# Row maximum of masked attention taken as a minimum of negatively scaled scores, signalled per tile

## The chip, the cores and the metric

The kernel runs on one NeuronCore of one Trainium2 chip. The metric is the device time of one execution in microseconds (us); lower is better.

## The reference, cut to what matters

Two transformer blocks run one after the other on 256 tokens of width 1024, in float32. They hold four attentions. Three are masked and hold 32 heads together: a causal block attention with 8 heads of 64 (`moba`), an attention over selected keys with 8 heads of 64 (`dsa`), and a latent attention with 16 heads of 96 (`mla`). The fourth, a cross attention with 4 heads of 256 (`cross`), has no mask. For each head and query the reference computes

```
logits = (q . k) * scale, masked entries -inf (or -1e30)
p      = softmax(logits)        # exp(logits - max) / sum
out    = p @ v
```

Around them lie projections, norms, retention, a short convolution and three feed-forward layers, which are matrix products against 176 MB of weights.

## The kernel before, in words

Each engine has a hand-written program, and semaphores order them. The 256 tokens are two tiles (t = 0, 1) of 128 rows. Weights stream through a ring: SyncE issues the loads (L379), ScalarE makes the rounded high part (`w_hi`, L572), VectorE the remainder (`w_lo`, L981 and L983), and TensorE multiplies three products of high and low parts (L1468). A weight unit's slot is released when TensorE has used it (`w_used`), and the raw slot when VectorE has made the low part (`w_low`).

An attention is a pipeline over heads, written once for all four (`attention` in each engine's program):

- TensorE: `scores(hd)` (L1572, one bank of PSUM, 128 columns for tile 0 and 256 for tile 1), then `turn_probs(hd-2)` (L1580, three transposes), then `values(hd-3)` (L1589, six products in the masked attentions). `scores(hd)` waits until the bank of head hd-2 is free (`maxed`).
- VectorE: `masked_max(hd)` makes two tensor_tensor_reduce (L1127), one for each tile: scores plus mask into the SBUF tile `S`, and the row maximum into `mx`. In the trace each is a CUSTOM_DVE_ANT_0 followed by a DVE_READ_ACCUMULATOR2_ANT. It then waits for its own two marks and makes the bias `nb = -scale * mx` for both tiles with one tensor_scalar of 2 columns (L1134, SBUF to SBUF), which raises `maxed` by 1. Behind it in the same queue stands `copy_turned(hd-2)` (L1140, PSUM to SBUF, 384 columns), on which `values` waits.
- ScalarE: for each head it waits on `maxed`, then makes `E = exp(scale * S + nb)` for tile 0 and tile 1 with row sums (L733), and signals `probs`. `turn_probs` waits on that.

In `moba` the first two heads stand inside a projection. ScalarE's program is: weight splits, head 0, one split (L572), the eviction of tile 0 (L631), head 1, the eviction of tile 1 (L631), then the other heads. VectorE's is: head 0, one split (L981), then the rest. TensorE waits for both evictions before `scores(3)`. In `mla` ScalarE has splits ahead of heads 2 and 4, VectorE ahead of heads 4 and 6. In `dsa` GpSimd runs the convolution at the same time (`convolve`, L500 to L504: tensor_tensor on SBUF tiles of 128x1024). Its result goes through ScalarE (L911) and VectorE (L1391) after the attention; TensorE's next projection waits for these.

The non-masked attention (`cross`) takes one tensor_reduce from PSUM (L1131) and the same tensor_scalar (L1134).

Of the kernel before, what the change touches and what calls it, by code (L numbers as in the profile page):

```python
# [19 lines left out]
ALU = mybir.AluOpType  # L20
# [5 lines left out]
TT = SEQ // P  # L26
# [3 lines left out]
PICKED = -3e38  # L30
# [65 lines left out]
def rows_stat(b, t):  # L96
    return added(b, t) + TT


def block_kernel(nc, A, out):  # L100

    with ExitStack() as ctx:
# [32 lines left out]
        PS = ctx.enter_context(nc.psum_tensor("PS", [P, 8, 512], F32))  # L135
# [63 lines left out]
        def out_banks(a, t):  # L199

            return PS[:, a.out_bank + t, :] if a.H * a.dv == 512 else acc(t).rearrange("p a b -> p (a b)")
# [354 lines left out]
        def _(act):  # L556
# [19 lines left out]
            def split_to(u):  # L576
                while n["split"] <= min(u, COUNT - 1):
                    split(n["split"])
                    n["split"] += 1

            def by_rows(stat):

                act.wait_ge(rstd_ready, stat + 1)
                return rstd[:, stat:stat + 1]
# [138 lines left out]
            def attention(a, heads=None, splits=True):  # L723
                for hd in heads or range(a.H):
                    if splits and hd in (2, 4):
                        split_to(min(n["split"], n["used"] + 1))
                    act.wait_ge(a.maxed, hd + 1)
                    if hd >= 3:
                        act.wait_ge(a.turned, hd - 2)
                    for t in range(TT):  # L730
                        c0, c1 = a.cols[t]
                        src = a.S[hd % 3][:, c0:c1] if a.masked else PS[:, a.score_bank + hd % 2, c0:c1]
                        ins = act.activation(a.E[hd % 3][:, c0:c1], src, ACT.Exp, bias=a.nb[:, hd, t:t + 1],  # L733
                                             scale=a.scale, accum_out=a.sums[:, hd, t:t + 1])
                    ins.then_inc(a.probs, 1)

            def whole(tile, width=512):
# [104 lines left out]
            n["used"] += 4  # L842
            split_to(n["used"] + 1)
            attention(moba, [0])
            split_to(n["used"] + 2)
            evict(0, rows2(k_tok), mem_rows)
            attention(moba, [1])
            evict(1, rows2(k_tok), mem_rows)
            attention(moba, range(2, moba.H), False)
            split_to(n["used"] + 3)  # L850
            high_banks(2, half_rows(hT_hi, 0))
# [71 lines left out]
            for t in range(TT):  # L923
                wait_acc(t)
                scale = by_rows(rows_stat(4, t))
# [40 lines left out]
        def _(dve):  # L966
            steps = Steps(dve, dve_step)
# [19 lines left out]
            def split_to(u):  # L987
                while n["split"] <= min(u, COUNT - 1):
                    split(n["split"])
                    n["split"] += 1  # L990
# [128 lines left out]
            def attention(a, heads=None, splits=True, rows=None):  # L1119
                def masked_max(hd):  # L1120
                    dve.wait_ge(a.scores, hd + 1)
                    if hd >= 3:
                        dve.wait_ge(a.probs, hd - 2)
                    if a.masked:
                        for t in range(TT):
                            c0, c1 = a.cols[t]
                            steps.mark(dve.tensor_tensor_reduce(  # L1127
                                out=a.S[hd % 3][:, c0:c1], in0=PS[:, a.score_bank + hd % 2, c0:c1], in1=a.mask[t], scale=1.0,
                                scalar=PICKED, op0=ALU.add, op1=ALU.max, accum_out=a.mx[:, hd, t:t + 1]))
                    else:  # L1130
                        steps.mark(dve.tensor_reduce(a.mx[:, hd, :], PS[:, a.score_bank + hd % 2, :].rearrange("p (t s) -> p t s", t=TT),  # L1131
                                                     AX, ALU.max))
                    steps.wait()
                    dve.tensor_scalar(a.nb[:, hd, :], a.mx[:, hd, :], -a.scale, None, ALU.mult).then_inc(a.maxed, 1)  # L1134

                def copy_turned(hd):
                    dve.wait_ge(a.turned, hd + 1)
                    if hd >= 2:
                        dve.wait_ge(a.summed, hd - 1)
                    dve.tensor_copy(a.ET[hd % 2], PS[:, a.prob_bank + hd % 2, 0:a.cols[1][1]]).then_inc(a.copied, 1)  # L1140

                for hd in heads or range(a.H + 2):
                    if splits and hd in (4, 6):
                        split_to(min(n["split"], n["used"] + 1))
                    if hd < a.H:
                        masked_max(hd)
                    elif rows is not None:
                        normalise_half(a, rows, hd - a.H, 0)
                    if hd >= 2:
                        copy_turned(hd - 2)  # L1150

            def normalise_half(a, dst, t, half):

                heads = slice(half * a.H // 2, (half + 1) * a.H // 2)
                if t == 0:
                    dve.wait_ge(a.summed, heads.stop)
                    steps.link(dve.reciprocal(a.sums[:, heads, :], a.sums[:, heads, :]))
                dve.tensor_tensor(dst[:, t, 512 * half:512 * half + 512].rearrange("p (h d) -> p h d", d=a.dv),
                                  PS[:, 2 * t + half, :].rearrange("p (h d) -> p h d", d=a.dv),
                                  a.sums[:, heads, t:t + 1].to_broadcast([P, a.H // 2, a.dv]), ALU.mult).then_inc(h_ready, 1)  # L1160
# [140 lines left out]
            for t in range(TT):  # L1301
                for hd in range(4):
                    cols, stat = slice(128 * hd, 128 * hd + 128), RETENTION + 4 * t + hd
                    ins = dve.scalar_tensor_tensor(out=mix[:, t, 512 + cols.start:512 + cols.stop], in0=PS[:, 2 + t, cols],
                                                   scalar=rstd[:, stat:stat + 1], in1=sil[:, t, cols], op0=ALU.mult, op1=ALU.mult)
# [98 lines left out]
            for t in range(TT):  # L1404
                dve.wait_ge(ss_ready, LATENTS + 2 * t + 2)
                s = rows_stat(4, t)
# [41 lines left out]
        def _(pe):  # L1448
# [115 lines left out]
            def attention(a, heads=None, rows=None):  # L1564
                def scores(hd):
                    if hd >= 2:
                        pe.wait_ge(a.maxed if a.masked else a.probs, hd - 1)
                    for t in range(TT):
                        c0, c1 = a.cols[t]
                        pairs = list(zip(a.q(hd, t * P, (t + 1) * P), a.k(hd, 0, c1 - c0)))  # L1570
                        for i, (q, k) in enumerate(pairs):
                            mm = pe.matmul(PS[:, a.score_bank + hd % 2, c0:c1], q, k, start=i == 0, stop=i == len(pairs) - 1)  # L1572
                    mm.then_inc(a.scores, 1)

                def turn_probs(hd):
                    pe.wait_ge(a.probs, hd + 1)
                    if hd >= 2:
                        pe.wait_ge(a.copied, hd - 1)
                    for b in range(a.cols[1][1] // P):
                        mm = pe.transpose(PS[:, a.prob_bank + hd % 2, b * P:(b + 1) * P], a.E[hd % 3][:, b * P:(b + 1) * P], ident[:])  # L1580
                    mm.then_inc(a.turned, 1)

                def values(hd):
                    pe.wait_ge(a.copied, hd + 1)
                    for t in range(TT):
                        c0, c1 = a.cols[t]
                        blocks = (c1 - c0) // P
                        for s in range(blocks):
                            mm = pe.matmul(out_banks(a, t)[:, hd * a.dv:(hd + 1) * a.dv], a.ET[hd % 2][:, c0 + s * P:c0 + (s + 1) * P],  # L1589
                                           a.v(hd, s), start=s == 0, stop=s == blocks - 1)  # L1590
                    mm.then_inc(a.summed, 1)

                for hd in heads or range(a.H + 3):
                    if hd < a.H:
                        scores(hd)
                    if 2 <= hd < a.H + 2:
                        turn_probs(hd - 2)
                    if hd >= 3:
                        values(hd - 3)
                    if rows is not None and hd == a.H + 1:  # L1600
                        turn_half(rows, 0)

            def turn_half(tile, at):

                for t in range(TT):
                    wait_h()
                    turn([tile[:, t, at + P * b:at + P * (b + 1)] for b in range(4)])
# [369 lines left out]
```

## Time and profile before

| what | value |
|---|---|
| median of 3 runs | 1088.29 us (1087.21 to 1093.13) |
| the profiled execution's own time | 1089.14 us |
| its span in the profile | 1087.3 us |
| granted TensorE clock, mean | 0.991 |
| TensorE (PE) matmul busy | 1044.9 us, 96% |
| VectorE (DVE) busy | 655.1 us, 60% |
| ScalarE (ACT) busy | 564.1 us, 52% |
| GpSimd (POOL) busy | 99.8 us, 9% |

The profile is of one execution. Times are us from the span's start unless marked ns. Busy time of matmuls is modelled from their starts, so 96% doesn't mean the peak rate. The span leaves out some 2 us around the program (1089.14 against 1087.3). The `moba` attention lies at 99 to 121 us, `dsa` at 550 to 572, `mla` at 841 to 873.

### The profile page before, as it was taken

Reading aid. Unit: us, or ns where it says so; the run is one execution under the profiler, and the core shown is the slowest. Engines: PE = TensorE matmul, PEld = TensorE weight load, DVE = VectorE, ACT = ScalarE, POOL = GpSimd, SP = SyncE. Lnnn points to the kernel's source line nnn. Section 1 sums busy time; section 2 is a strip of 40 time slices with the busy share of each in tenths; the row PEclk is TensorE's granted clock in tenths of the full one; section 3 lists DMA queues with packets and bytes.
Section 4 is the critical chain, followed back from the end, with each engine's and each line's share of the span. In section 5 each row is a group of like instructions: output and inputs, shape, how many; then the busy total and the mean of one; then the engine's idle time right before and its main releaser. Section 6 shows DMA issues by size and latency. Waiting matters only on the chain.

```text
span 1087.3 us, 13860 instructions
## 1 busy us (share of the span) xinstructions
PE 1044.9 (96%) x5080; PEld 872.4 (80%) x5080; DVE 655.1 (60%) x1020; ACT 564.1 (52%) x855; POOL 99.8 (9%) x127
## 2 busy tenths in 40 slices
PE   7999999999999999999979999999997999999997
PEld 6887878887888887878867888888886878888886
DVE  5575665456565555647876755545654867555453
ACT  6566455437454455644544744454454647445541
POOL 2010110001000001104440100000140001000000
PEclk9999999999999999999989999999999999999999
DMA  8746136215545545633422655554252225555521
GB/s 336 279 174 230 58 117 219 110 58 183 204 159 190 215 149 187 237 136 118 152 75 103 234 188 196 188 192 153 70 190 105 78 92 221 191 195 190 193 78 39
DMA packets 28462, 176.31 MB, mean 162 GB/s; under 512 B 3248, under 2 KB 3392, under 8 KB 9984
## 3 DMA queue, kind: packets, MB, share of 16 engines
q1 hardware_dynamic: 26784, 170.08, 43.2%
q0 software_dynamic: 1456, 5.48, 1.4%
q8 instruction: 30, 0.49, 0.2%
q10 hardware_dynamic: 176, 0.13, 0.0%
q14 instruction: 16, 0.13, 0.0%
HBM read 174.62 MB, written 1.05 MB: 162 GB/s over the span
## 4 chain that ended last, share of the span: by engine, by line
PE 82%; DVE 9%; ACT 3%; issue 3%; POOL 2%; DMA 1%; SPq 0%; DVEq 0%; ACTq 0%; POOLq 0%
PE PS L1468 71%; PE PS L1537 3%; DVE w_lo L983 3%; PE PS L1589 2%; PE PS L1572 2%; ACT w_hi L572 2%; PE PS L1679 2%; DVE w_lo L981 1%; DMA x<-in_x 1%; DVE work L1127 1%; POOL h L487 1%; PE PS L1580 1%; DVE h L1347 1%; POOL arena L480 1%; ACT work L653 0%
## 5 line engine op out<-in xcount | busy, mean ns | idle before, releaser
L983 DVE SCALAR_TENSOR_TENSOR w_lo<-w_raw,gcol,w_hi 128x512 fp32r<-128x512 f32 (+4 forms) x322 | 269.4, 895 | 208.4 <-ACT w_hi L572 207.8
L572 ACT ACTIVATE w_hi<-w_raw,gcol 128x512 fp32r<-128x512 f32 (+4 forms) x322 | 243.4, 824 | 99.4 <-PE PS L1468 98.5
L1468 PE MATMUL PS<-w_hi,hT_hi 128*128 128x512 f32 (+3 forms) x904 | 246.4, 393 | 7.8 <-DVE hT_lo L998 3.0
L1468 PE MATMUL PS<-w_hi,hT_lo 128*128 128x512 f32 (+3 forms) x904 | 240.2, 386 | 0.0
L1468 PE MATMUL PS<-w_lo,hT_hi 128*128 128x512 f32 (+3 forms) x904 | 238.9, 385 | 0.9 <-DVE w_lo L983 0.8
L1468 PEld LDWEIGHTS PS<-w_lo,hT_hi 128*128 128x128 f32 x904 | 167.5, 188 | 35.9 <-DVE w_lo L983 2.4
L1468 PEld LDWEIGHTS PS<-w_hi,hT_hi 128*128 128x128 f32 x904 | 164.0, 189 | 40.1 <-issue 3.8
L1468 PEld LDWEIGHTS PS<-w_hi,hT_lo 128*128 128x128 f32 x904 | 168.1, 189 | 33.2
L981 DVE TENSOR_TENSOR w_lo<-w_raw,w_hi 128x2048 fp32r<-128x2048 f32 (+1 forms) x70 | 135.7, 1954 | 83.7 <-ACT w_hi L572 83.6
L572 ACT ACTIVATE w_hi<-w_raw 128x2048 fp32r<-128x2048 f32 (+1 forms) x70 | 114.6, 1644 | 106.7 <-PE PS L1468 106.7
L1468 PE MATMUL PS<-w_hi,gT_hi 128*128 128x512 f32 x408 | 113.9, 392 | 0.0
L1468 PE MATMUL PS<-w_lo,gT_hi 128*128 128x512 f32 x408 | 112.9, 390 | 0.0
L1468 PE MATMUL PS<-w_hi,gT_lo 128*128 128x512 f32 x408 | 112.7, 389 | 0.0
L463 POOL TENSOR_SCALAR msq<-ssq 128x1 f32<-128x1 f32 (+1 forms) x31 | 13.0, 418 | 856.1 <-ACT work L653 792.5
L1468 PEld LDWEIGHTS PS<-w_hi,gT_lo 128*128 128x128 f32 x408 | 76.6, 188 | 16.0
L1468 PEld LDWEIGHTS PS<-w_lo,gT_hi 128*128 128x128 f32 x408 | 76.5, 188 | 15.9
L1468 PEld LDWEIGHTS PS<-w_hi,gT_hi 128*128 128x128 f32 x408 | 76.2, 188 | 15.5
L591 ACT ACTIVATE hT_hi<-PS 128x512 fp32r<-128x512 f32 (+1 forms) x46 | 25.3, 582 | 46.1 <-PE PS L1537 46.1
L998 DVE TENSOR_TENSOR hT_lo<-PS,hT_hi 128x512 fp32r<-128x512 f32 (+1 forms) x46 | 29.4, 669 | 31.3 <-ACT hT_hi L591 31.1
L631 ACT ACTIVATE arena<-PS,rstd 128x1024 f32<-128x1024 f32 (+1 forms) x22 | 22.8, 1036 | 44.7 <-PE PS L1468 30.7
L733 ACT ACTIVATE work<-work,attention_bias 128x128 f32<-128x128 f32 x64 | 28.5, 446 | 31.2 <-DVE attention_bias L1134 31.2
L1572 PE MATMUL PS<-arena 128*128 128x256 f32 (+1 forms) x160 | 37.9, 369 | 5.7 <-DVE attention_bias L1134 2.2
(151 smaller groups left out, 786.0 us busy)
## 6 DMA issues: line engine op xcount, KB each, us to landing
w_raw<-in_w SPq DMA_DIRECT2D x64, 1024.0 KB, 4.8
w_raw<-in_w_gu SPq DMA_DIRECT2D x22, 1024.0 KB, 4.8
w_raw<-in_w_in SPq DMA_DIRECT2D x11, 1024.0 KB, 7.6
w_raw<-in_w_dn SPq DMA_DIRECT2D x22, 512.0 KB, 5.4
w_raw<-in_w_mem_k SPq DMA_DIRECT2D x4, 1024.0 KB, 4.9
w_raw<-in_w_out SPq DMA_DIRECT2D x4, 1024.0 KB, 4.8
w_raw<-in_w_cq SPq DMA_DIRECT2D x4, 1024.0 KB, 4.7
w_raw<-in_w_mem_v SPq DMA_DIRECT2D x4, 1024.0 KB, 4.8
```

What stands on the lines that cost most here:

```text
L572: ins = act.activation(w_hi[:, u % RING, k * w:(k + 1) * w], w_raw[:, u % RAW, k * w:(k + 1) * w], ACT.Copy, scale=1.0 if col is None else ...
L591: act.activation(d, PS[:, 4 + n["tb"] % 4, 0:blocks * P].rearrange("p (b m) -> p b m", m=P), ACT.Copy).then_inc(tb_high, 1)
L631: ins = act.activation(dst, src, ACT.Copy, scale=scale)
L733: ins = act.activation(a.E[hd % 3][:, c0:c1], src, ACT.Exp, bias=a.nb[:, hd, t:t + 1], scale=a.scale, accum_out=a.sums[:, hd, t:t + 1])
L981: ins = dve.tensor_tensor(lo, raw, hi, ALU.subtract)
L983: ins = dve.scalar_tensor_tensor(out=lo, in0=raw, scalar=gcol[:, col + TURNED * k:col + TURNED * k + 1], in1=hi, op0=ALU.mult, op1=ALU.sub ...
L998: dve.tensor_tensor(lo, PS[:, 4 + n["tb"] % 4, 0:blocks * P].rearrange("p (b m) -> p b m", m=P), hi.bitcast(F32), ALU.subtract).then_inc(t ...
L1468: mm = pe.matmul(bank(t, j)[:, 0:width], rows[:, kc0 + k, tok], w[:, s, at:at + width], start=begin and i == 0, stop=end and i == 2)
L1537: mm = pe.transpose(PS[0:rows, 4 + n["tb"] % 4, i * P:(i + 1) * P], src, ident[:])
L1572: mm = pe.matmul(PS[:, a.score_bank + hd % 2, c0:c1], q, k, start=i == 0, stop=i == len(pairs) - 1)
L1589: mm = pe.matmul(out_banks(a, t)[:, hd * a.dv:(hd + 1) * a.dv], a.ET[hd % 2][:, c0 + s * P:c0 + (s + 1) * P], a.v(hd, s), start=s == 0, st ...
L1679: mm = pe.transpose(m.turn_bank[t][:, b * P:(b + 1) * P], hidden[:, t, b * P:(b + 1) * P], ident[:])
```

## The change

For the masked attentions the reduction scales by `-scale` and takes the minimum, starting from the negated start value; its result goes straight into `nb`. The tensor_scalar and the wait ahead of it are left out. `S` now holds `-scale * (score + mask)`, so that ScalarE takes the exponential with scale -1.0. `maxed` is raised by each tile's reduction, so twice for each head; ScalarE waits for each tile ahead of that tile's exponential, and TensorE waits for twice the count. The attention without a mask keeps its instructions.

```diff
--- before.py
+++ after.py
@@ -724,14 +724,17 @@
                 for hd in heads or range(a.H):
                     if splits and hd in (2, 4):
                         split_to(min(n["split"], n["used"] + 1))
-                    act.wait_ge(a.maxed, hd + 1)
+                    if not a.masked:
+                        act.wait_ge(a.maxed, hd + 1)
                     if hd >= 3:
                         act.wait_ge(a.turned, hd - 2)
                     for t in range(TT):
+                        if a.masked:
+                            act.wait_ge(a.maxed, TT * hd + t + 1)
                         c0, c1 = a.cols[t]
                         src = a.S[hd % 3][:, c0:c1] if a.masked else PS[:, a.score_bank + hd % 2, c0:c1]
                         ins = act.activation(a.E[hd % 3][:, c0:c1], src, ACT.Exp, bias=a.nb[:, hd, t:t + 1],
-                                             scale=a.scale, accum_out=a.sums[:, hd, t:t + 1])
+                                             scale=-1.0 if a.masked else a.scale, accum_out=a.sums[:, hd, t:t + 1])
                     ins.then_inc(a.probs, 1)
 
@@ -1124,14 +1127,13 @@
                     if a.masked:
                         for t in range(TT):
                             c0, c1 = a.cols[t]
-                            steps.mark(dve.tensor_tensor_reduce(
-                                out=a.S[hd % 3][:, c0:c1], in0=PS[:, a.score_bank + hd % 2, c0:c1], in1=a.mask[t], scale=1.0,
-                                scalar=PICKED, op0=ALU.add, op1=ALU.max, accum_out=a.mx[:, hd, t:t + 1]))
+                            dve.tensor_tensor_reduce(
+                                out=a.S[hd % 3][:, c0:c1], in0=PS[:, a.score_bank + hd % 2, c0:c1], in1=a.mask[t], scale=-a.scale,
+                                scalar=-PICKED, op0=ALU.add, op1=ALU.min, accum_out=a.nb[:, hd, t:t + 1]).then_inc(a.maxed, 1)
                     else:
-                        steps.mark(dve.tensor_reduce(a.mx[:, hd, :], PS[:, a.score_bank + hd % 2, :].rearrange("p (t s) -> p t s", t=TT),
+                        steps.link(dve.tensor_reduce(a.mx[:, hd, :], PS[:, a.score_bank + hd % 2, :].rearrange("p (t s) -> p t s", t=TT),
                                                      AX, ALU.max))
-                    steps.wait()
-                    dve.tensor_scalar(a.nb[:, hd, :], a.mx[:, hd, :], -a.scale, None, ALU.mult).then_inc(a.maxed, 1)
+                        dve.tensor_scalar(a.nb[:, hd, :], a.mx[:, hd, :], -a.scale, None, ALU.mult).then_inc(a.maxed, 1)
 
@@ -1564,7 +1566,10 @@
             def attention(a, heads=None, rows=None):
                 def scores(hd):
                     if hd >= 2:
-                        pe.wait_ge(a.maxed if a.masked else a.probs, hd - 1)
+                        if a.masked:
+                            pe.wait_ge(a.maxed, TT * (hd - 1))
+                        else:
+                            pe.wait_ge(a.probs, hd - 1)
                     for t in range(TT):
```

## Rows read from the trace of the kernel before

**Rows 1.** The page: the chain that ended last, share of the span by engine.
```profile
PE 82%; DVE 9%; ACT 3%; issue 3%; POOL 2%; DMA 1%; SPq 0%; DVEq 0%; ACTq 0%; POOLq 0%
```

**Rows 2.** Instructions of L1127 and L1134: duration ns min/median/max, first and last start.
```profile
L1127 DVE CUSTOM_DVE_ANT_0 work<-PS,causal x48: 281/356/421, 99.8 to 868.2; 128x128 f32<-128x128 f32 x24, 128x256 f32<-128x256 f32 x24
L1134 DVE TENSOR_SCALAR attention_bias<-attention_max x36: 169/170/1847, 100.5 to 868.6; 128x2 f32<-128x2 f32 x36
```

**Rows 3.** One head at full pace in dsa: three pieces of the chain, then timeline.
```profile
565.44 0.71 PE PS L1572 x4
566.15 0.33 PE PS L1580 x3
566.47 0.62 PE PS L1589 x6
...
566.86 0.17 DVE L1134 TENSOR_SCALAR attention_bias<-attention_max 128x2 f32<-128x2 f32 x1
566.94 0.56 DVE L1140 COPY work<-PS 128x384 f32<-128x384 f32 x1
567.07 0.40 ACT L733 ACTIVATE work<-work,attention_bias 128x128 f32<-128x128 f32 x1 [0.67 <-DVE attention_bias L1134]
567.84 0.29 DVE L1127 CUSTOM_DVE_ANT_0 work<-PS,h 128x128 f32<-128x128 f32 x1 [0.34 <-PE PS L1572]
567.87 0.19 ACT L733 ACTIVATION_READ_ACCUMULATOR work<-work,attention_bias 128x1 f32 x1
```

**Rows 4.** Timeline of dsa, 550 to 570 us: GpSimd's convolution and VectorE's instructions.
```profile
550.33 2.90 PE L1572 MATMUL PS<-arena 128*128 128x128 f32 x8 [0.87 <-DVE arena L1016]
552.20 0.08 DVE L1127 DVE_READ_ACCUMULATOR2_ANT attention_max<- 128x1 f32 x1
552.20 0.42 DVE L1127 CUSTOM_DVE_ANT_0 work<-PS,h 128x256 f32<-128x256 f32 x1
552.33 1.89 POOL L502 TENSOR_TENSOR arena<-arena,conv_w 128x1020 f32<-128x1020 f32 x1
552.66 1.59 DVE L1134 TENSOR_SCALAR attention_bias<-attention_max 128x2 f32<-128x2 f32 x1
...
554.83 1.85 DVE L1134 TENSOR_SCALAR attention_bias<-attention_max 128x2 f32<-128x2 f32 x1
...
558.55 0.55 DVE L1140 COPY work<-PS 128x384 f32<-128x384 f32 x1
...
560.76 2.36 POOL L504 TENSOR_TENSOR arena<-arena 128x1024 f32<-128x1024 f32 x1
```

**Rows 5.** Windows of dsa: length, busy of PE, PEld, DVE, ACT, POOL, granted clock, DMA.
```profile
556.00:558.00 2.00, 1.27 (x4) 1.16 (x5) 1.97 (x6) 0.98 (x4) 1.92 (x2) 0.68 0.00 0
560.00:562.00 2.00, 2.00 (x9) 1.71 (x9) 1.16 (x2) 0.99 (x4) 1.92 (x2) 0.50 0.00 0
564.00:566.00 2.00, 2.00 (x17) 1.80 (x16) 1.28 (x6) 0.75 (x5) 0.00 (x0) 1.00 0.00 0
```

**Rows 6.** The chain in dsa: scores of heads 4, 5 and 7.
```profile
560.70 1.39 PE PS L1572 x4
...
563.78 0.71 PE PS L1572 x4
...
567.09 0.72 PE PS L1572 x4
```

**Rows 7.** Timeline of moba's entry.
```profile
100.70 0.40 ACT L733 ACTIVATE work<-work,attention_bias 128x128 f32<-128x128 f32 x1 [3.70 <-DVE attention_bias L1134]
...
103.53 2.29 DVE L981 TENSOR_TENSOR w_lo<-w_raw,w_hi 128x2048 fp32r<-128x2048 f32 x1 [2.86 <-ACT w_hi L572]
...
108.65 0.92 PE L1572 MATMUL PS<-arena 128*128 128x128 f32 x4 [1.75 <-ACT h L631]
```

**Rows 8.** Timeline of mla's entry.
```profile
846.50 2.29 DVE L981 TENSOR_TENSOR w_lo<-w_raw,w_hi 128x2048 fp32r<-128x2048 f32 x1
...
854.72 0.88 PE L1589 MATMUL PS<-arena,work 128*128 128x64 f32 x6 [1.07 <-DVE work L1140]
```

## The prediction, made before the result was known

> **What bounds the kernel now.** I read the chain of work first: TensorE carries 82% of it, VectorE 9%, ScalarE 3% [rows 1]. A change to VectorE pays only where TensorE waits for it. So I read the three masked attentions one by one, first at full pace, then at their entries and exits.
>
> At full pace a head costs TensorE 0.71 us of scores, 0.33 of transposes and 0.62 of values, 1.66 together [rows 3]. VectorE is idle 0.34 us in that period and waits for TensorE; ScalarE is idle 0.67 us and waits for the bias [rows 3]. There TensorE is the bound, and the small bias instruction is covered.
>
> Where heads come slower, the cover is gone. In `dsa` the bias instruction on two columns, 0.17 us in the median and 1.847 at most [rows 2], took 1.59 us and then 1.85 us [rows 4]. The first ended at 552.66 + 1.59 = 554.25, just behind GpSimd's L502, which ended at 552.33 + 1.89 = 554.22. The pattern stands five times (heads 0 to 4, the last one held only 0.18 us): the instruction ends 0.02 or 0.03 us after a convolution step of GpSimd. VectorE's other work isn't held: the masked reduction of 256 columns took 0.42 us and the copy of 384 columns 0.55 us while GpSimd was busy [rows 4]. So the bias instruction alone, both sides in SBUF, waits for GpSimd. `maxed` hangs on it, and on that both the exponential and the scores two heads on. TensorE idled, its granted clock fell to 0.50, the level of 1.2 GHz, and came back to 1.00, 2.4 GHz, only after a stretch of unbroken work [rows 5].
>
> **The change, part by part.** The sum is made in the profiled execution (1089.14 us, span 1087.3), which is 0.85 us over the median of 1088.29; I take the difference off the median.
>
> *dsa.* Today the scores of heads 0 and 1 run from 550.33 for 2.90 us, to 553.2 [rows 4]. That is half pace: eight instructions at 0.71 us for four would take 1.4. The first reduction's maximum is there at 552.20 + 0.08 = 552.28, the second's at 552.20 + 0.42 = 552.62 [rows 4]. After the change both semaphores stand by 552.65, ahead of the end of head 1's scores, so TensorE goes straight on to head 2 at 553.2. Exponentials of head 0 take 0.99 us from the first start to the last sum (567.07 to 567.87 + 0.19 [rows 3]), so from 552.33 to 553.3, ahead of TensorE's need. Then: scores and transposes of heads 2 and 0, 0.71 + 0.33 = 1.04, and four rounds of 1.66 for heads 3 to 6, 6.64. Head 7's scores start at 553.2 + 1.04 + 6.64 = 560.9 instead of 567.09 [rows 6]. **Gain 6.2 us.** This takes the full clock for granted from about 553.3 on. Today it was granted by then: the mean of 0.68 over 556 to 558 [rows 5] can only come from a stretch that began at 1.00 and fell to 0.50 inside it. The copy for head 0 ends at about 555.2, just ahead of its use at 555.3, so this entry has no room for more. Next in line is the convolution. GpSimd's last step ends at 560.76 + 2.36 = 563.1 [rows 4], and VectorE's part of it would start, behind the last copy, at about 564.8. It stays covered by some 0.4 us, ScalarE's first conversion between them counted. If it were uncovered, little more would be lost than what the attention gained beyond it, so this is the low end of the time, not a loss.
>
> *moba.* Two gains in series, each of the same kind. A head's first exponential can start 0.05 us after the first maximum (552.28), where today it starts 0.05 after a bias that is unhindered (552.62 + 0.04 + 0.17 = 552.83 [rows 2, 4]): 0.55 us earlier. Head 0's exponentials start at 100.15 instead of 100.70; behind them in ScalarE's queue stands the weight split that VectorE's split at 103.53 waited for [rows 7], and behind VectorE's split stands head 1's reduction. That comes 0.55 earlier, its exponentials 1.1 earlier, and the eviction behind them too, for which TensorE idled 1.75 us at 108.65 [rows 7]. So 1.1 of 1.75. I take **1.05**. Its bounds are 0, if another wait ends the same stretch (the slot of the weights, the projection's end), and 1.1.
>
> *mla.* Head 0's exponentials end 0.55 earlier, so ScalarE's split and with it VectorE's at 846.50 [rows 8] start 0.55 earlier. After it VectorE works without a pause through heads 4 and 5 and the next split, until TensorE, idle 1.07 us for a copy at 854.72 [rows 8], has its work. There each bias left out is time on the path: its start, 0.04 after the maximum, and the 0.08 until the next instruction starts behind it (566.86 to 566.94 [rows 3]), 0.12 each, for heads 4, 5 and 6. 0.55 + 0.36, with some reordering at the entry: **0.95**. Bounds 0.36 and 1.07.
>
> *Exits.* In each attention the last head's reduction stands ahead of the copy for two heads before, on which TensorE waits. One bias less, 0.12 each, **0.35** for three. Bounds 0 and 0.21 each (0.17 + 0.04).
>
> *Costs.* ScalarE gets one more wait for each of 32 heads. Waits aren't rows of their own. From below it costs nothing; from above I set 0.08 us, the shortest thing that a VectorE accumulator read takes [rows 4], for each head, inside ScalarE's idle 0.67 [rows 3]: 0 at full pace and under 0.3 us at the entries; I take 0. If that cover were gone it would be 32 x 0.08 = 2.6. The reduction itself keeps its shape; the minimum in place of the maximum and a scale other than 1 are not shown by any row. The nearest row is the reduction as it is, 281 to 421 ns [rows 2]; I take that, and price a slower one below. The mirrored numbers and ScalarE's scale of -1.0 change no size. No transfer moves: SyncE's loads hang on `w_low`, which comes earlier by what each attention gains.
>
> Sum: 6.2 + 1.05 + 0.95 + 0.35 = 8.55 us. 1088.29 - 8.55 = **1079.7 us**.
>
> The Trainium skill, "SBUF — State Buffer", section "Who interferes with whom", says that VectorE and GpSimd share one pair of SBUF interfaces under an exclusive lock, which a tensor_scalar can need and an instruction with one SBUF input and PSUM for the other doesn't. By that rule the masked reduction stays free of GpSimd, and the sum is as above. It also names instructions with two SBUF inputs as held while GpSimd reads; here that is VectorE's part of the convolution (L1391), which comes only after GpSimd has ended, so it adds nothing.
>
> **The rivals.**
>
> *The clock stays low in dsa.* TensorE is idle ahead of 550, and its clock was 0.50 at 560 to 562 although it was busy for all of that [rows 5]. If it stays at 0.50 until about 563.5, as today, a head costs 563.78 - 560.70 = 3.08 us [rows 6]. From 553.2, scores and transposes of heads 2 and 0 take about 2.0; heads 3 to 5 end near 564, and head 7's scores start at about 565.9, a gain of 1.2 instead of 6.2: 1084.7 us. Against it: today the clock had come back by 556 on the same work that stands ahead of 553.2 in the changed kernel, and it fell again within 556 to 558 [rows 5], after pauses of TensorE that the bias instructions of 1.59 and 1.85 us had made, and these go. The Trainium skill, "TensorE: Matmul & The Clock Gate", section "HAM oscillation — how this bites in real kernels", describes this very loss, pauses that bring the slow clock back; and it calls the moment of a switch variable between runs, which speaks for some scatter here.
>
> *The hold goes to the next instruction of VectorE.* Then dsa gains nothing but its exit, and 2.35 us are left: 1085.9. Against it stand the 0.42 and 0.55 us under a busy GpSimd [rows 4].
>
> *Only dsa gains.* If at both other entries another wait ends the stretch: 6.2 + 0.35, 1081.7 us. The entries were walked through only queue by queue.
>
> *Slower: the new reduction runs below one column for about 1 ns.* Today 128 more columns cost 421 - 281 = 140 ns [rows 2], so both tiles stream 0.42 us a head. VectorE's room at full pace is 0.34 + 0.12 = 0.46 us. Beyond that each head pays: some 22 heads at pace and 6 on the path. With d us more for a head the change costs 22 (d - 0.46) + 6 d; it eats 8.55 at d = 0.67, when streaming takes 2.6 times as long. At four times, d = 1.26, it costs 17.6 + 7.6 = 25.2: 1104.9 us. For it speaks only that the operation is another one; against it, that its form, two inputs and one running value, is the same.
>
> *The change has no effect*, because ScalarE's and TensorE's waits end on something else: 1088.
>
> **How the numbers follow.** Forecast 0.70; clock stays low 0.11; only dsa 0.08; hold moves 0.04; no effect 0.04; slower 0.03. The least that a measurement of this kernel can tell from no change is about 0.5%, 5.4 us, so faster means below 1082.8. Forecast and "only dsa" are faster, 0.78; low clock, moved hold and no effect are the same, 0.19; slower 0.03. The forecast's own ends are 1077.6 and 1082. The low one: moba's and mla's upper bounds, 0.17 more, 0.3 more at the exits, 0.5 for a walk in dsa made by hand, and the 1.08 us by which the lowest run lay under the median. The high one: moba 0 and mla 0.36 give 1081.3, and 0.7 for the walk. Up to 1084.7 it takes in the low clock, and leaves out about 0.11.
>
> **What would show it.** After: no rows on the bias instruction but the 4 of `cross`; exponentials starting about 0.33 us after a head's reduction starts; in dsa full clock from about 553, no pause of TensorE over 0.3 us between 550 and 565, scores every 1.66 us, attention ending 6 us sooner; GpSimd's steps as long as now; the pause of 1.75 in moba down to about 0.7. Wrong would be: reductions over 0.45 us for 256 columns, a reduction held next to a GpSimd step, or a clock of 0.50 in dsa beyond 557.

## The result and the profile after

The changed kernel took **1083.07 us** in the median of 8 runs (1081.68 to 1085.15), the kernel before 1088.74 in as many (1087.21 to 1093.13). The ratio is 0.9939, with a 95% interval of 0.9925 to 0.9953: 0.6% faster, a gain of 5.7 us. Forecast were 1079.7 and 8.55 us. The time lies 1.1 us above 1082, the upper end that the forecast gave itself, and inside the range up to 1084.7, which takes in the rival of a clock that stays low. It is also 0.3 us above 1082.8, where the prediction put the least change that can be told from none; the interval excludes no change all the same. The profiled execution of the changed kernel took 1082.35 us (span 1080.6), 6.8 less than the profiled one before, in which the sum had been made.

The page of the changed kernel: its span, busy time by engine, and the chain by engine. Beside [rows 1], VectorE's share of the chain is 8% in place of 9%, and 32 instructions are gone.

```profile
span 1080.6 us, 13828 instructions
PE 1042.8 (97%) x5080; PEld 872.5 (81%) x5080; DVE 644.9 (60%) x988; ACT 564.0 (52%) x855; POOL 99.7 (9%) x127
PE 83%; DVE 8%; ACT 3%; issue 3%; POOL 2%; DMA 1%; SPq 0%; DVEq 0%; ACTq 0%; POOLq 0%
```

The reduction's own line in the changed kernel (duration ns min/median/max, first and last start, forms), to be read against [rows 2]. The minimum with a scale costs what the maximum cost, 280/356/422 against 281/356/421.

```profile
L1130 DVE CUSTOM_DVE_ANT_0 work<-PS,causal x48: 280/356/422, 100.6 to 861.7; 128x128 f32<-128x128 f32 x24, 128x256 f32<-128x256 f32 x24
L1130 DVE DVE_READ_ACCUMULATOR2_ANT attention_bias<- x64: 82/83/86, 100.8 to 862.0; 128x1 f32 x64
```

The timeline of `dsa` in the changed kernel (start, length, engine, line, operation, in brackets the idle time before it and what ended it), beside [rows 4]:

```profile
550.38 4.18 PE L1577 MATMUL PS<-arena 128*128 128x128 f32 x12 [0.87 <-DVE arena L1019]
552.26 0.42 DVE L1130 CUSTOM_DVE_ANT_0 work<-PS,h 128x256 f32<-128x256 f32 x1
552.38 0.40 ACT L736 ACTIVATE work<-work,attention_bias 128x128 f32<-128x128 f32 x1 [1.93 <-DVE attention_bias L1130]
552.39 1.89 POOL L502 TENSOR_TENSOR arena<-arena,conv_w 128x1020 f32<-128x1020 f32 x1
...
554.36 0.85 PE L1585 MATMUL PS<-ident,work 128*128 128x128 f32 x3
...
560.81 2.36 POOL L504 TENSOR_TENSOR arena<-arena 128x1024 f32<-128x1024 f32 x1
...
561.61 0.88 PE L1577 MATMUL PS<-arena 128*128 128x128 f32 x4
...
566.89 1.20 PE L1470 MATMUL PS<-w_hi,hT_hi 128*128 128x512 f32 x4 [0.46 <-DVE hT_lo L1393]
```

The reader is to see three things. The scores of heads 0 to 2 are one unbroken run of 12 instructions where TensorE had paused after 8. ScalarE starts 0.34 us after the reduction of tile 0, which began at 552.04. GpSimd's steps are as long as before (1.89 and 2.36 us). But 12 instructions of scores took 4.18 us, half pace for all three heads.

The windows of the changed kernel say why (length, busy time of PE, PEld, DVE, ACT and POOL, granted clock, DMA share, GB/s), beside [rows 5]:

```profile
548.00:550.00 2.00, 1.51 (x8) 0.93 (x6) 1.48 (x3) 1.43 (x2) 0.00 (x0) 0.56 0.78 274
552.00:554.00 2.00, 2.00 (x9) 1.68 (x8) 1.29 (x8) 1.33 (x6) 1.92 (x2) 0.50 0.00 0
554.00:556.00 2.00, 2.00 (x12) 1.71 (x11) 1.30 (x6) 1.63 (x8) 1.92 (x2) 0.73 0.00 0
556.00:558.00 2.00, 2.00 (x19) 1.90 (x17) 1.46 (x8) 1.04 (x5) 1.92 (x2) 1.00 0.00 0
```

The clock was at 0.50, the level of 1.2 GHz, from 548.2 to 555.1, through the transposes ahead of the attention and its first heads, and then stayed at 1.00.

**Where the time went.** I measure each attention from the first scores of head 0 to the first matmul of what follows it. That removes the different starts: head 0 of `moba` began at 98.96 before and 99.78 after, and anywhere from 97.93 to 99.78 in the ten traces of this study, although nothing had been changed ahead of it.

| stretch | before | after | gain | forecast |
|---|---|---|---|---|
| start to `moba` | 98.96 | 99.78 | -0.82 | 0 |
| `moba` | 21.22 | 19.91 | 1.31 | 1.17 |
| `moba`'s end to `dsa` | 430.15 | 430.69 | -0.54 | 0 |
| `dsa` | 22.08 | 16.51 | 5.57 | 6.32 |
| `dsa`'s end to `mla` | 268.58 | 268.78 | -0.20 | 0 |
| `mla` | 32.45 | 31.09 | 1.36 | 1.07 |
| `mla`'s end to the end | 213.86 | 213.84 | 0.02 | 0 |

(The forecast's 0.12 for each exit is counted with its attention.) Each stretch is read from one execution of either kernel. The three attentions gained 8.24 us together, against 8.56 forecast. The stretches between gave 1.54 back.

### The profile page after: what moved, and what is told of

Same layout as the page of the kernel before. It is cut to its first block, busy times and chain, and to the rows that moved or that the text cites. A ratio compares the mean times of both kernels' runs of the same rounds, so it can differ in the third digit from the quotient of the medians.

```text
span 1080.6 us, 13828 instructions
## 1 busy us (share of the span) xinstructions
PE 1042.8 (97%) x5080; PEld 872.5 (81%) x5080; DVE 644.9 (60%) x988; ACT 564.0 (52%) x855; POOL 99.7 (9%) x127
## 3 DMA queue, kind: packets, MB, share of 16 engines
HBM read 174.62 MB, written 1.05 MB: 163 GB/s over the span
## 4 chain that ended last, share of the span: by engine, by line
PE 83%; DVE 8%; ACT 3%; issue 3%; POOL 2%; DMA 1%; SPq 0%; DVEq 0%; ACTq 0%; POOLq 0%
PE PS L1470 72%; PE PS L1539 3%; DVE w_lo L986 3%; PE PS L1577 2%; PE PS L1594 2%; ACT w_hi L572 2%; PE PS L1684 2%; DVE w_lo L984 1%; PE PS L1585 1%; DMA x<-in_x 1%; POOL h L487 1%; DVE h L1349 1%; POOL arena L480 1%; ACT work L653 0%; DVE arena L1019 0%
## 5 line engine op out<-in xcount | busy, mean ns | idle before, releaser
L1064 DVE TENSOR_TENSOR work<-PS,gain 128x512 f32<-128x512 f32 x28 | 18.0, 686 | 42.2 <-ACT work L653 42.2
L653 ACT ACTIVATE work<-PS 128x1024 f32<-128x1024 f32 x14 | 14.4, 1027 | 52.3 <-PE PS L1470 52.3
```

What stands on the lines that cost most here:

```text
L1064: steps.mark(dve.tensor_tensor(work[:, 2 * t + i, :], PS[:, 2 * t + i, :], gain[:, g, cols], ALU.mult))
```

## The experiments

Eight kernels ran, the first four (one-column form, signal by head, the two short convolutions) on one chip and the other four on another, each time beside the kernel before. That took 1089.40 us in the first group and 1089.58 in the second, and the ratios are to it. The stretches come from one execution each. Line numbers are those of each kernel.

### Does the number of columns decide the hold?

One-column bias instructions, the old arithmetic, in the frame of the changed kernel:

```diff
-dve.tensor_tensor_reduce(..., scale=-a.scale, scalar=-PICKED, op1=ALU.min, accum_out=a.nb[:, hd, t:t + 1]).then_inc(a.maxed, 1)
+steps.mark(dve.tensor_tensor_reduce(..., scale=1.0, scalar=PICKED, op1=ALU.max, accum_out=a.mx[:, hd, t:t + 1]))
+for t in range(TT):
+    dve.wait_ge(steps.s, steps.n - 1 + t)
+    dve.tensor_scalar(a.nb[:, hd, t:t + 1], a.mx[:, hd, t:t + 1], -a.scale, None, ALU.mult).then_inc(a.maxed, 1)
```

> The changed kernel with the old arithmetic put back in one-column pieces: reduction by maximum into mx, then for each tile its own tensor_scalar of one column, each with its own signal. Length of dsa from head 0's scores to the projection's first matmul was 22.1 us before and 16.5 after. Theory 1 (the two-column instruction was held because it is cut in two halves that use both of VectorE's SBUF paths, one of them shared with GpSimd): one column cannot be cut, so no instruction is held; each takes 0.06 to 0.2 us, dsa takes 16.5 to 17.8 us, the time is 1083 to 1085. Theory 2 (any small SBUF to SBUF instruction of VectorE is held while GpSimd works): the one-column instructions last up to 1.8 us and end with GpSimd's steps, dsa takes 20 to 23 us, the time is 1087 to 1090.

Measured: 1084.3 us, ratio 0.9956 (0.9940 to 0.9973). `dsa` 17.39, `moba` 20.94, `mla` 32.30. The instruction's line in this kernel, and one place of its timeline with GpSimd busy beside it:

```profile
L1135 DVE TENSOR_SCALAR attention_bias<-attention_max x64: 148/152/155, 99.3 to 862.7; 128x1 f32<-128x1 f32 x64
551.03 1.89 POOL L502 TENSOR_TENSOR arena<-arena,conv_w 128x1020 f32<-128x1020 f32 x1
...
551.24 0.27 DVE L1135 TENSOR_SCALAR attention_bias<-attention_max 128x1 f32<-128x1 f32 x2
```

None of the 64 took more than 155 ns, where the two-column form took up to 1847 [rows 2]. Theory 1 holds: the same operation on the same tiles is held with two columns and free with one. Cutting one instruction in two, with the signals by tile, had 4.69 of the 5.57 us in `dsa`. Part of the 0.88 that is missing is clock: the stretch at 0.50 covered 6.1 us of this kernel's `dsa` and 4.7 of the changed kernel's. In `moba` and `mla` the one-column form had only 0.28 and 0.15, since two bias instructions stand there where there was one. The Trainium skill, "SBUF — State Buffer", section "Who interferes with whom", gives the rule behind it (VectorE in a mode that uses both interface pairs waits for the whole of GpSimd's instruction, otherwise not, if it has one SBUF input); the trace agrees: with two columns the instruction ends just behind GpSimd's. The pairs as such are in no row; the dependence on the column count is.

### What do the signals by tile bring?

```diff
-                        if a.masked:
-                            act.wait_ge(a.maxed, TT * hd + t + 1)
+                    act.wait_ge(a.maxed, hd + 1)        # once for each head
...
-                            dve.tensor_tensor_reduce(...).then_inc(a.maxed, 1)
+                            ins = dve.tensor_tensor_reduce(...)
+                        ins.then_inc(a.maxed, 1)
```

> The changed kernel, but with one signal for each head, raised by the second tile's reduction, and one wait on ScalarE. Theory 1 (in dsa the instruction that is gone did it; the signals by tile only help at the entries of moba and mla): dsa stays within 0.5 us of 16.5; from head 0's scores to the end of moba's last values it loses some 0.6 of the 1.31 us that moba gained, mla some 0.3 of its 1.36; the time is 1083.5 to 1085. Theory 3 (starting the first tile's exponential early is the main part): dsa goes back to 19 us or more and the time above 1086.

Measured: 1083.54 us, ratio 0.9936 (0.9912 to 0.9960), not to be told from the changed kernel by its time. By stretches: `moba` 20.61 (0.70 of its 1.31 lost), `mla` 31.43 (0.34 of 1.36), `dsa` 17.07. That is 0.56 us over the changed kernel's, a little more than the 0.5 that I allowed; but 5.8 us of it lay at the low clock, which lasted to 559.8, against 4.7 us there. Theory 1 holds, with its sizes at the two entries; theory 3 wanted 19 us. Signalling each tile is worth about 1 us in the traces, at the two entries, too little to show between the medians.

### Is it GpSimd that held the instruction?

In the kernel before and in the changed one, the convolution was cut to one product; its taps and their sums are left out.

```diff
-                for shift in range(3):
-                    ...
-                pool.tensor_tensor(y_conv, y_conv, gbT, ALU.mult).then_inc(conv_ready, 1)
+                pool.tensor_tensor(y_conv, uT, gbT, ALU.mult).then_inc(conv_ready, 1)
```

> The kernel before, with GpSimd's convolution cut to one product of 128x1024 (the taps and their sums are left out), so that GpSimd is idle from about 2 us after head 0's scores start. Theory 1: every bias instruction of dsa takes 0.17 us, and dsa takes 16.6 to 18 us instead of 22.1, with the bias instructions still there; the time is 1082 to 1085. Theory 4 (the small instruction waits for something other than GpSimd): they stay at 1 to 1.85 us and dsa at 22.

> The changed kernel with the same one product in place of the convolution. Theory 1: nothing of VectorE was held any more, so dsa stays at 16.5 us within 0.3 apart from where the clock's dip falls, and the time is within 2 us of the changed kernel's. A rival: the convolution's end at 563 still bound the end of dsa; then dsa is shorter by more than 0.5 us at the same clock.

Measured: the kernel before with the short convolution 1084.57 us, ratio 0.9953 (0.9938 to 0.9969), `dsa` 16.33; the changed kernel with it 1082.5, ratio 0.9937 (0.9912 to 0.9961), `dsa` 14.72. The bias instruction in the first of them:

```profile
L1125 DVE TENSOR_SCALAR attention_bias<-attention_max x36: 168/169/170, 100.5 to 864.2; 128x2 f32<-128x2 f32 x36
```

Its maximum fell from 1847 to 170 ns, and `dsa` from 22.08 to 16.33, with every bias instruction in place. It was GpSimd. (I had expected at least 16.6; it was 0.3 less. Some of the fall is clock: 3.2 us of this `dsa` lay at 0.50, against 9.8 us in the kernel before.) The second run missed my figure: I expected 16.5, and it was 14.72. Its trace has no stretch of low clock in `dsa` at all. Its 12 scores, and two of its windows:

```profile
551.54 2.55 PE L1568 MATMUL PS<-arena 128*128 128x128 f32 x12 [0.87 <-DVE arena L1010]
```

```profile
552.00:554.00 2.00, 1.92 (x11) 1.31 (x11) 1.29 (x8) 1.19 (x6) 1.92 (x1) 1.00 0.45 188
554.00:556.00 2.00, 2.00 (x17) 1.77 (x16) 1.87 (x10) 2.00 (x11) 0.00 (x0) 1.00 0.00 0
```

That left two readings, the clock or the convolution's end, and called for the next two kernels.

### The clock

Idle transposes of the identity go into a bank that nobody reads, in TensorE's two pauses ahead of `dsa` (2.38 and 0.87 us long in the changed kernel), so that it has work there. First in the changed kernel, then in the kernel before:

```diff
+            def fill(count, bank):
+                for _ in range(count):
+                    pe.transpose(PS[:, bank, 0:P], ident[:], ident[:])
...
             turn_parts((vg_tok, 512))
+            pe.wait_ge(acc_copied, n["copied"] - 1)
+            fill(20, 0)
             turn_half(cx_tok, 0)
+            fill(7, 0)
             turned(4)
             attention(dsa)
```

> The changed kernel with idle transposes of the identity (20 and 7, into a bank that nobody reads) put in TensorE's two pauses ahead of dsa, so that it is not idle there. Theory C (what dsa gained less than forecast is the slow clock granted from 548 to 555 us): no stretch at 0.50 begins between 545 and 560, dsa takes 14.7 us instead of 16.5, as it did in the execution without the convolution that had no slow stretch, and about 0.5 us less goes into the transposes ahead of it; the time is about 1.5 to 2.5 us under the changed kernel's, 1080.5 to 1082. Theory D (TensorE waits in dsa for something else, the copies or ScalarE): dsa stays at 16 us or more at full clock. The fillers cost up to 0.4 us if they run over the pause.

> The kernel before with the same idle transposes. It splits the 22.1 us of dsa into the hold and the clock. Theory C with theory 1: the bias instructions are still held to the ends of GpSimd's steps, the first heads still come one for each step, so dsa takes 20 to 21.5 us although it begins at full clock; TensorE's pauses between 553 and 557 can bring the slow clock on again. The time is 1087 to 1089. If the clock were the cause and not the hold, dsa would fall to 17 us or less.

Measured, changed kernel with the filling: 1080.77 us, ratio 0.9910 (0.9893 to 0.9927), `dsa` 14.77. Its timeline and windows:

```profile
546.40 2.35 PE L1550 MATMUL PS<-ident 128*128 128x128 f32 x20
...
550.07 0.93 PE L1550 MATMUL PS<-ident 128*128 128x128 f32 x7
551.10 2.55 PE L1581 MATMUL PS<-arena 128*128 128x128 f32 x12
```

```profile
549.00:551.00 2.00, 1.99 (x15) 1.57 (x15) 1.90 (x3) 1.32 (x2) 0.00 (x0) 1.00 0.90 238
551.00:553.00 2.00, 1.82 (x10) 1.40 (x11) 0.95 (x7) 1.19 (x4) 1.87 (x1) 1.00 0.68 287
553.00:555.00 2.00, 2.00 (x15) 1.61 (x15) 1.64 (x10) 2.00 (x10) 1.92 (x2) 1.00 0.00 0
```

The 12 scores take 2.55 us in place of 4.18. Theory C holds: 14.7 expected, from the execution without the convolution, and 14.77 found, with the whole convolution beside it. So the convolution's end binds nothing (14.72 without it), and the low clock cost the changed kernel 16.51 - 14.77 = 1.74 us in `dsa`. The medians, 1080.77 and 1083.07, come from two chips.

The kernel before with the filling: 1087.64 us, ratio 0.9987 (0.9972 to 1.0002), `dsa` 19.52. I had expected 20 to 21.5 us there. It started at full clock and stayed at 1.00 through all of `dsa`, and the bias instruction was held all the same, in six of the eight heads:

```profile
551.76 1.90 POOL L502 TENSOR_TENSOR arena<-arena,conv_w 128x1020 f32<-128x1020 f32 x1
...
552.28 1.40 DVE L1134 TENSOR_SCALAR attention_bias<-attention_max 128x2 f32<-128x2 f32 x1
...
553.73 2.35 POOL L503 TENSOR_TENSOR arena<-arena 128x1020 f32<-128x1020 f32 x1
...
554.26 1.85 DVE L1134 TENSOR_SCALAR attention_bias<-attention_max 128x2 f32<-128x2 f32 x1
...
556.62 0.88 PE L1593 MATMUL PS<-arena,work 128*128 128x64 f32 x6 [1.32 <-DVE work L1140]
```

This splits the 5.57 us of `dsa`. At full clock on both sides the hold and the instruction itself are worth 19.52 - 14.77 = 4.75. The other 0.82 is clock: it cost 22.08 - 19.52 = 2.56 before and 1.74 after. In this execution pauses of TensorE of up to 1.32 us, behind held instructions, brought no low clock. A second slow stretch, well inside `dsa`, came in two of the three executions with held instructions (the kernel before and the one of the next section) and in none of the seven without. So the prediction's reading that the hold also brings the low clock [rows 5] fits, but not in every execution.

### Through the wait or through the queue?

```diff
                            ...accum_out=a.nb[:, hd, t:t + 1]).then_inc(a.maxed, 1)
+                        dve.wait_ge(a.maxed, TT * (hd + 1))
+                        dve.tensor_scalar(a.mx[:, hd, :], a.nb[:, hd, :], 1.0, None, ALU.mult)
```

> The changed kernel with a two-column tensor_scalar put back behind each head's two reductions, for whose result nobody waits (nb into the unused mx). Theory 1: it is held in dsa to the end of GpSimd's step as before, 1 to 1.85 us, and with it the next reduction and the copy that stand behind it in VectorE's queue, while the exponentials and scores two heads on go at once; dsa takes 19 to 21 us instead of 16.5, so most of the old loss went through the queue. Theory 5 (the loss went through the wait on maxed): dsa stays under 18 us although the instruction is held. Outside dsa some 0.1 us for each entry and exit. The time is 1085 to 1088 by theory 1, 1083 to 1085 by theory 5.

Measured: 1089.04 us, ratio 0.9987 (0.9977 to 0.9998), `dsa` 21.66, `moba` 20.12, `mla` 31.94. The timeline of this kernel:

```profile
553.49 1.89 POOL L502 TENSOR_TENSOR arena<-arena,conv_w 128x1020 f32<-128x1020 f32 x1
...
553.82 1.58 DVE L1134 TENSOR_SCALAR attention_max<-attention_bias 128x2 f32<-128x2 f32 x1
...
555.32 0.28 DVE L1130 CUSTOM_DVE_ANT_0 work<-PS,h 128x128 f32<-128x128 f32 x1
...
560.30 0.88 PE L1596 MATMUL PS<-arena,work 128*128 128x64 f32 x6 [3.05 <-DVE work L1144]
```

An instruction whose result nobody reads takes back 5.15 of the 5.57 us. Some of that is clock again: 6.7 us of this `dsa` lay at 0.50, in two stretches, against 4.7 us in the changed kernel. Head 1's reduction, whose scores were ready, starts at 555.32, only when the held instruction is through, and TensorE idles 3.05 us for a copy that stands behind three of them. Theory 1 holds: the loss went through VectorE's queue, while in this kernel nothing waits for the held instruction itself. The time lies 1 us over my range of 1085 to 1088: `dsa` took 21.66 us, a little over the 21 expected, and `mla` lost 0.85 us, where I had expected some 0.1 for each entry and exit.

### A version that beats both

The same filling at two more pauses:

```diff
+            def filled_heads():
+                pe.wait_ge(acc_copied, n["copied"])
+                fill(26, 2)
+                wait_h(2)
+                turn_heads(1)
...
-            project(1, 2, wide, kc0=3, copies=2, rows=latents, hooks={(1, 0): after_h(lambda: turn_heads(1), 2)})
+            project(1, 2, wide, kc0=3, copies=2, rows=latents, hooks={(1, 0): filled_heads})
...
                 turn_half(mix, 512)
+                fill(11, 2)
                 turned(2)
```

> The changed kernel with idle transposes at three places: ahead of dsa as in f, 26 in the 3.3 us pause ahead of the second half of the latent queries (at 814), and 11 behind the last turn ahead of the second feed of retention (at 136). Theory C: slow stretches near 138, 548 and 817 are gone, each of 3.4 us at half clock costs up to 1.7 us where TensorE is the bound, so the time is 1 to 3 us under f, 1078 to 1081. A rival: the slow clock there falls on work that waits for other engines anyway, then nothing is won over f.

Measured: **1077.76 us** (1075.25 to 1080.27), ratio 0.9887 (0.9865 to 0.9910) to the kernel before, so 1.1% faster and 3 us under the filling at `dsa` alone, whose interval overlaps a little. It is 0.2 us under my range. The median hides two groups: three executions of 1075.3 to 1075.6 us with a mean granted clock of 0.999, and three of 1079.9 to 1080.3 with 0.995 or 0.996; the five of the kernel filled at `dsa` only took 1080.1 to 1081.5 at 0.994. The profiled execution is of the first group, with a span of 1073.8 us and no low clock before the kernel's last 3 us. At the long pause ahead of the latent queries:

```profile
809.20 3.00 PE L1550 MATMUL PS<-ident 128*128 128x128 f32 x26
812.69 1.95 PE L1539 MATMUL PS<-ident,h 128*96 128x128 f32 x16 [0.50 <-DVE h L1051]
```

and the same transposes in the changed kernel without the filling:

```profile
817.90 3.60 PE L1539 MATMUL PS<-ident,h 128*96 128x128 f32 x16 [3.34 <-DVE h L1051]
```

1.95 us in place of 3.60 for the same 16. From `dsa`'s end to `mla` it took 267.16 us against 268.81 in the kernel filled at `dsa` only: 1.65 for one slow stretch. From `moba`'s end to `dsa` it took 428.58 against 431.79 there, which had slow stretches near 138 and 462: 1.6 for each. The one at 462 has no filling near it, and it was missing in this execution and in the changed kernel's. So a part of this trace's lead is scatter. The medians, 3.0 us apart, are the fairer figure, though with two groups of three a rough one.

## Why the prediction was right, and by how much it missed

**The bound and the hold.** Right. Full pace is 1.66 us a head before and after, and the bias instruction costs nothing there. In `dsa` it waited for GpSimd, because it is small, from SBUF to SBUF and two columns wide. I had argued this from the times at which it ended; the short convolution and the one-column form show it.

**dsa, 6.2 and 0.12 at the exit.** The mechanism was right; the term was mis-sized, at 5.57. The step that failed was "This takes the full clock for granted from about 553.3 on". I placed the slow stretch of the changed kernel where it had been before, 549.9 to 553.3. It came at 548.2 and lasted to 555.1. At full clock the stretch is 14.77 us long; my walk meant 22.08 - 6.32 = 15.76, which is that and 1.0 for the slow stretch that I kept. It cost 1.74. The rest of the walk stands: TensorE went from head to head without a pause, and fell to the slow clock no more once it had left it.

**moba, 1.05 and 0.12; mla, 0.95 and 0.12.** 1.31 and 1.36, so 0.14 and 0.29 too low. The reading queue by queue was right in kind. In `moba` TensorE's pause for the eviction at 108.36 fell from 1.75 to 0.64 us, by 1.11 where I gave 1.05 to 1.1. In `mla` the pause for the copy was to close but for 0.1; it fell only from 1.07 to 0.67, and the pauses ahead of it, which I had not counted, fell from 1.51 to 0.85 us together. Both pauses stand in the timeline of the changed kernel, beside [rows 7, 8]:

```profile
108.36 0.92 PE L1577 MATMUL PS<-arena 128*128 128x128 f32 x4 [0.64 <-ACT h L631]
...
848.25 0.88 PE L1594 MATMUL PS<-arena,work 128*128 128x64 f32 x6 [0.67 <-DVE work L1142]
```

That the three attentions came to 8.24 us, close to the 8.56 forecast, is partly luck: 0.75 too much in `dsa` stands against 0.43 too little in the other two.

**What lay between.** Forecast as nothing, it took back 1.54 us in the traces: 0.82 ahead of any change, and 0.74 in two stretches. For 0.54 of these the slow stretches account: without any, 428.58; one near 461 before, 1.6, makes 430.2 (found 430.15); one near 138 and the slow transposes ahead of `dsa` (547.79 to 550.38, 2.59 us, where it was 2.13 before) make 428.58 + 1.6 + 0.46 = 430.6 (found 430.69). For 0.20 I have no account.

**The median.** The profiled executions are 6.8 us apart, the medians 5.7, and the interval of the ratio, 5.1 to 8.2 us in this kernel's time, leaves my 8.55 out by little. One slow stretch is worth 1.6 us. Where it falls changes from execution to execution, so a forecast made in one trace carries an error of this size. My upper end of 1082 had 0.7 us for the walk in `dsa` and nothing for a slow stretch elsewhere, which was too little.

**The rivals.** The clock that stays low in `dsa` was half right: lower for longer than I forecast, but not to 563.5, and it cost 0.7 us of the gain and not 5. The hold did not go to the next instruction: the reduction kept 356 ns in the median and 422 at most. Nor was there a slower reduction, or no effect. That only `dsa` gains is refuted by 1.31 and 1.36 us elsewhere. The wait that I had added to ScalarE at no cost did cost nothing that can be seen: it starts 0.04 us after the accumulator is read.

## What to carry to other kernels

Look for small VectorE instructions whose longest time is ten times their median, and hold their ends against GpSimd's: a two-column instruction from SBUF to SBUF can be held until GpSimd's instruction ends, here for up to 1.85 us, and all that stands behind it in VectorE's queue waits too. Take such an instruction out, or cut it so that it runs on one column, before GpSimd's work is moved. Then look at TensorE's pauses of 1 to 3 us ahead of a dense stretch: here idle transposes of 0.11 us each at three places took the ratio to the kernel before from 0.9939 to 0.9887, about as much again as the change itself.

## What the runs showed of the hardware that I had not expected

Behind pauses of TensorE of 2.4 to 3.3 us a stretch at 0.50 followed in most executions, 3.4 or 6.8 us long: ahead of the latent queries, where the pause is 3.3 us, in all nine without the filling there, and at `dsa` in six of seven. The work that it slows need not stand next to the pause. With the pause filled there was none, in the three kernels filled at `dsa` and in the one at the latent queries. Near 138 five of nine had one without filling; one execution with it settles nothing there.

TensorE can fall to the slow clock without any pause. In the kernel before it did so at 461.1 (start and end, length, matmul busy, granted clock, DMA share, GB/s):

```profile
459.00:461.00 2.00, 2.00 (x21) 1.00 0.45 94
461.00:463.00 2.00, 2.00 (x7) 0.53 0.99 418
463.00:465.00 2.00, 2.00 (x7) 0.61 0.85 291
```

Just ahead of it stand 48 matmuls of 80 columns in place of 512, back to back at 0.11 us each, as here in the kernel before:

```profile
456.53 1.07 PE L1468 MATMUL PS<-w_hi,hT_lo 128*128 128x80 f32 x8
457.43 1.06 PE L1468 MATMUL PS<-w_lo,hT_hi 128*128 128x80 f32 x8
```

The trace counts TensorE as busy throughout, yet in eight of the ten executions profiled the clock fell during these 48 matmuls or within 0.4 us behind them. In the changed kernel's and in the one filled at all three places it did not. No kernel here changed these matmuls, so the cause stays open.
